# A hybrid decoder layer on one core: the first weight chunk loaded in two parts behind two tiles of x, ScalarE's and VectorE's opening work in another order

## Chip, cores and metric

One NeuronCore of a Trainium2 chip. The metric is the device time of one execution in microseconds; the time before is the median of three runs.

## What is computed

One inference step of a decoder layer, in fp32, for 512 prompt rows and 8 sample rows of width 1024:

```python
xn = rms_norm(x, g_norm_mix)
z = xn @ w_in                      # 1024 x 3072: q 768 | k 768 | v 768 | B 256 | C 256 | u 256
q, k = rope(rms_norm(heads(q), g_q), pos), rope(rms_norm(heads(k), g_k), pos)
# attention over three dilated windows, short convolution of C * u, one output projection
h = x + concat([attn_out, conv_out]) @ w_out
y = h + hier_moe(rms_norm(h, g_norm_ffn))     # top 1 of 4 groups, top 2 of 8 experts, 32 experts
```

The change lies in the first tenth of the time: the norm of x, its transposition, and the first columns of `xn @ w_in`.

## The kernel before

Each engine has its own program, written out by hand; the engines meet at semaphores, and each works strictly in its own order. Names: `pe` is TensorE, `act` ScalarE, `dve` VectorE, `pool` GpSimd, `sp` the queue that issues loads.

**Opening.** x comes as the sample rows (tile NT) and four tiles of 128 rows (0 to 3). For a tile, ScalarE squares and takes the root (`x_square`), VectorE scales (`x_scale`), TensorE transposes eight blocks of 128 x 128 in two halves, VectorE multiplies by the gain out of the bank (`x_whole(g)`). The halves are counted g = 1 to 8, g = 0 being the sample rows: tile t has g = 2t + 1 and 2t + 2. The products are made of two reduced-precision parts: ScalarE copies a part `xT_high` (`x_high(g)`), and the difference `xT_low` is made by VectorE for g = 1 to 4 (`x_low`) and by GpSimd for 5 to 8 (L1811). The difference takes the place of the whole value.

**Projection.** `w_in` is cut into 8 chunks of 384 columns, `wchunk[c]`, loaded in one transfer each. A chunk is split as x is: ScalarE copies `w_high` in four pieces (`high(c, i)`, two of the eight row blocks each), VectorE subtracts to `w_low` (`low(c, i)`), in place over the chunk, so not before `partial_sums(c)` has read it for the sample rows. Per chunk and tile, a unit, TensorE does 16 matmuls with `w_high` (`by_high`, L670 and L671) and 8 with `w_low` (L694). Chunks 0 and 1 are q, 2 and 3 are k. Units of these four go through a norm and rotation: ScalarE squares (L1090), VectorE reduces (L1351), ScalarE roots, VectorE scales and multiplies by the cosine table, GpSimd multiplies by the sine table (L1837) and adds (L1853), TensorE turns the result back (`turn_rot`) three units later. VectorE makes the low pieces of chunk c + 1 between its units of chunk c. The tables `rope_g` hold cosine and sine times the gain, two for q and two for k, and VectorE makes all of them ahead of its first unit (L1337, L1340).

**Sample rows.** `partial_sums(c)` gives sums in four strips that `part_copy` (ScalarE) and `combine` (TensorE) bring together. `turn_state` transposes the convolution's state into bank 4; ScalarE copies it (`cu_s`, L1113) before `combine(0)` writes that bank.

**Loads.** `sp` issues, in this order: sample rows, tile 0, identity, gains, tiles 1 to 3, chunk 0, cosine and sine tables and small constants (`misc_in`), chunks 1 and 2. Later chunks wait for units to be done, and expert weights (L484, L492, L497) for the work that frees their slots.

Of the kernel before, what the change touches and what calls it, by code (L numbers as in the profile page):

```python
# [26 lines left out]
P = 128  # L27
# [10 lines left out]
CW = 384  # L38
# [87 lines left out]
def build(nc, x_prompt, x_sample, cache_k, cache_v, state_conv, g_norm_mix, w_in, g_q, g_k, w_conv, g_attn_out,  # L126
# [3 lines left out]
    with ctx:  # L130
# [119 lines left out]
        def sm(name):  # L250
# [10 lines left out]
        gqk = cut(work, 3200, 2, DH)  # L261
# [42 lines left out]
            y_ready y_out  moved_go dve_link act_link pool_link flag_ready zero_rows gu_front gu_half""".split()  # L304
# [81 lines left out]
        def _(sp):  # L386
# [13 lines left out]
            sp.dma_start(wchunk[0], w_in_v[:, :, 0:CW]).then_inc(w_in_s[0], 16)  # L400
# [134 lines left out]
            half_gates((30, 31), 0, 0, S["gu_front"])  # L535
# [33 lines left out]
        def _(pe):  # L569
# [5 lines left out]
            for g in range(2 * NT + 1):  # L575
                t, half = (g - 1) // 2, (g - 1) % 2
                pe.wait_ge(S["x_scaled"], t + 2)
                if g >= 3:
                    pe.wait_ge(S["x_whole"], g - 2)
                if g == 0:  # L580
                    for k in range(KD):
                        last = pe.transpose(bank[g % 3][:, k * DEC:(k + 1) * DEC], xn[0:DEC, NT, k * P:(k + 1) * P],
                                            ident[0:DEC, 0:DEC])
                else:
                    for k in range(4):
                        o = (4 * half + k) * P
                        last = pe.transpose(bank[g % 3][:, k * P:(k + 1) * P], xn[:, t, o:o + P], ident[:, :])
                last.then_inc(S["x_turned"], 1)
            pe.wait_ge(S["x_whole"], 2 * NT + 1)
# [62 lines left out]
            def partial_sums(c):  # L652

                pe.wait_ge(w_in_s[c % 4], 16 * (c // 4 + 1))
                if c >= 1:
                    pe.wait_ge(S["part_evac"], c)
                for k in range(KD):
# [5 lines left out]
            def by_high(c, t):  # L663
# [3 lines left out]
                if c == 0:  # L667
                    pe.wait_ge(S["x_evac"] if t < 2 else S["x_evac_p"], 2 * (t % 2) + 2)
# [4 lines left out]
            partial_sums(0)  # L673
            pend = []
            for c in range(QKV_CHUNKS):
                pe.wait_ge(S["w_high_done"], 4 * (c + 1))
                if c == 0:
                    by_high(0, 0)
                    by_high(0, 1)
                    turn_state()  # L680
                for t in range(NT):
# [9 lines left out]
                    if t == 0:  # L691
                        pe.wait_ge(S["w_low_done"], 4 * (c + 1))
# [3 lines left out]
                    last.then_inc(S["z_done"], 1)  # L696
                    if t == 0 and c <= 4 or (c, t) == (5, 2):
# [32 lines left out]
            for i in range(6):  # L730
# [11 lines left out]
                if i % 3 == 0:  # L742
                    pe.wait_ge(S["w_low_done"], 4 * (c + 1))
# [141 lines left out]
            def keep_warm(n):  # L885

                for _ in range(n):
                    pe.matmul(bank[2][:, 0:P], ident[:, :], ident[:, :], start=True, stop=True)

# [67 lines left out]
            keep_warm(13)  # L957
            count(2)
            keep_warm(9)
            tabulate(2)  # L960
            keep_warm(16)


            def pair(i, s, turn, first, split=False):
# [6 lines left out]
                pe.wait_ge(*((S["gu_front"], 64) if split else (gu_in[s], loads)))  # L971
# [68 lines left out]
        def _(act):  # L1040
# [16 lines left out]
            def high(c, i):  # L1057

                act.wait_ge(w_in_s[c % 4], 16 * (c // 4 + 1))
# [3 lines left out]
            x_square(NT)  # L1063
            x_square(0)
            x_square(1)
            for t in (2, 3):
                x_high(2 * t - 3)
                x_high(2 * t - 2)
                x_square(t)
            x_high(5)  # L1070
            x_high(6)
            for i in range(4):
                high(0, i)
            x_high(7)
            x_high(8)

            def part_copy(c):
# [3 lines left out]
                act.activation(partial, bank[3][:, 0:CW], ACT.Copy).then_inc(S["part_evac"], 1)  # L1081

# [11 lines left out]
            part_copy(0)  # L1094
            k = 0
            pend = []
            for c in range(QKV_CHUNKS):
                for t in range(NT):
# [11 lines left out]
                    if (c, t) == (0, 0):  # L1110
                        act.wait_ge(S["state_turned"], 1)
                        for h in range(2):
# [845 lines left out]
```

## Time and profile before

| | |
|---|---|
| median of three runs | 631.76 us (626.87 to 632.2) |
| profiled execution | 633.07 us |
| its span | 631.4 us |
| TensorE busy | 87% |
| VectorE, ScalarE, GpSimd busy | 43%, 26%, 18% |
| mean granted clock of TensorE | 0.941 |

A busy share is a mean over the whole span; the opening has other shares than the rest. The span runs from the first to the last instruction, and the execution's own time is somewhat longer.

### The profile page before, as it was taken

What the parts mean: (1) busy time and instruction counts of PE and PEld (TensorE: products, weight loads), DVE (VectorE), ACT (ScalarE), POOL (GpSimd) and SP (SyncE); (2) the same over time, 40 slices, a digit from 0 to 9 for tenths busy, and PEclk for the clock granted to TensorE, in tenths of its full rate; (3) what the DMA queues carried; (4) which work ended last, traced back from release to release, by engine and by line L of the source; (5) the groups of instructions that cost most, each with busy time, mean ns of one, the idle gap of its engine ahead of it and who ended that gap; (6) DMA issues with size and microseconds to landing.
All of it is one profiled execution on the core that took longest, in us unless ns stands there. A gap on an engine that the chain in (4) does not pass through costs nothing.

```text
span 631.4 us, 8032 instructions
## 1 busy us (share of the span) xinstructions
PE 548.1 (87%) x2894; PEld 330.8 (52%) x2894; DVE 271.2 (43%) x628; ACT 161.3 (26%) x357; POOL 113.5 (18%) x126
## 2 busy tenths in 40 slices
PE   3799999998998999899999889999987869787920
PEld 3588899896764887754555743333322323232300
DVE  4876686978313687534266722111210201111117
ACT  5543444423301557520322311010100101000000
POOL 0367788510000000000000131111110111100000
PEclk9699999999999999889999889999997979897985
DMA  7872332589449300049502929999999999999628
GB/s 267 265 195 101 103 137 89 165 244 309 161 125 333 144 1 2 2 195 422 223 33 94 373 70 364 420 418 418 421 421 422 420 419 421 420 422 410 245 75 349
DMA packets 42805, 159.71 MB, mean 253 GB/s; under 512 B 8800, under 2 KB 18080, under 8 KB 30968
## 3 DMA queue, kind: packets, MB, share of 16 engines
q1 hardware_dynamic: 36400, 143.85, 59.9%
q0 software_dynamic: 6368, 15.38, 6.9%
q8 instruction: 21, 0.34, 0.2%
q14 instruction: 16, 0.13, 0.1%
HBM read 151.59 MB, written 16.03 MB: 265 GB/s over the span
## 4 chain that ended last, share of the span: by engine, by line
PE 55%; SPq 17%; DMA 13%; DVE 6%; ACT 3%; issue 2%; POOL 2%; POOLq 0%; DVEq 0%; ACTq 0%
SPq L484 11%; PE bank L976 10%; PE bank L924 9%; SPq L497 5%; DMA ring<-in_w_up_dram 5%; PE bank L1003 4%; PE bank L807 4%; PE bank L694 3%; DMA x<-q_rows 3%; PE bank L670 3%; PE bank L671 3%; PE bank L718 2%; PE bank L792 2%; DMA ring<-results 2%; PE bank L659 2%
## 5 line engine op out<-in xcount | busy, mean ns | idle before, releaser
L976 PE MATMUL bank<-ring,work 128*64 128x512 f32 x512 | 124.3, 642 | 22.7 <-DMA ring<-in_w_up_dram 21.2
L976 PEld LDWEIGHTS bank<-ring,work 128*64 128x64 f32 x512 | 40.0, 148 | 105.1 <-issue 88.0
L1274 DVE TENSOR_TENSOR work<-work,bank 128x256 f32<-128x256 f32 x16 | 6.7, 421 | 140.5 <-ACT work L1243 140.5
L670 PE MATMUL bank<-split 128*128 128x384 f32 x192 | 66.5, 346 | 0.0
L1003 PE MATMUL bank<-ring,work 128*64 128x512 f32 x256 | 58.5, 598 | 7.6 <-ACT work L1247 7.6
L671 PE MATMUL bank<-split 128*128 128x384 f32 x192 | 64.6, 336 | 0.0
L1274 DVE TENSOR_TENSOR split<-ring,split 128x768 fp32r<-128x768 f32 (+1 forms) x36 | 39.6, 1138 | 8.3 <-PE bank L659 8.3
L924 PE MATMUL bank<-ring 128*128 128x512 f32 x96 | 42.6, 594 | 0.0
L1243 ACT ACTIVATE work<-bank 128x256 f32<-128x256 f32 x16 | 6.1, 384 | 140.9 <-PE bank L976 140.9
L1837 POOL TENSOR_TENSOR ring<-ring 128x192 f32<-128x192 f32 (+1 forms) x40 | 37.6, 960 | 17.6 <-DVEq L1362 16.2
L1866 POOL DMA_DIRECT2D hn_rows<-work x5 | 2.7, 543 | 210.6 <-ACT work L1229 210.6
L670 PEld LDWEIGHTS bank<-split 128*128 128x128 f32 x192 | 36.4, 189 | 3.2 <-issue 1.3
L694 PE MATMUL bank<-split 128*128 128x384 f32 x192 | 37.5, 336 | 0.1
L1189 ACT ACTIVATE ring<-ring,st 128x512 f32<-128x512 f32 (+3 forms) x48 | 26.5, 554 | 43.4 <-DVE st L1440 43.4
L1003 PEld LDWEIGHTS bank<-ring,work 128*64 128x64 f32 x256 | 17.0, 136 | 38.8 <-issue 27.4
L671 PEld LDWEIGHTS bank<-split 128*128 128x128 f32 x192 | 36.4, 190 | 0.0
L1888 POOL DMA_INDIRECT results<-work,tbl x16 | 16.1, 1004 | 112.8 <-DVE work L1727 112.8
L1727 DVE COPY work<-bank 128x512 f32<-128x512 f32 x16 | 11.1, 692 | 55.2 <-PE bank L1003 55.2
L694 PEld LDWEIGHTS bank<-split 128*128 128x128 f32 x192 | 33.5, 188 | 1.1 <-issue 0.6
L1880 POOL DMA_INDIRECT work<-hn_rows,tbl x16 | 16.1, 1009 | 98.9 <-PE bank L987 86.8
L1631 DVE SCALAR_TENSOR_TENSOR x<-bank,st,x 128x512 f32<-128x512 f32 (+1 forms) x20 | 15.0, 748 | 37.2 <-PE bank L924 27.6
L807 PE MATMUL bank<-ring 128*128 128x64 f32 x240 | 30.4, 274 | 0.4 <-DVE ring L1274 0.3
(219 smaller groups left out, 808.1 us busy)
## 6 DMA issues: line engine op xcount, KB each, us to landing
ring<-in_w_down_dram SPq DMA_DIRECT2D x32, 1024.0 KB, 24.9
ring<-in_w_gate_dram SPq DMA_DIRECT2D x28, 1024.0 KB, 23.7
ring<-in_w_up_dram SPq DMA_DIRECT2D x28, 1024.0 KB, 25.7
ring<-in_w_in_dram SPq DMA_DIRECT2D x8, 1536.0 KB, 10.4
x<-in_x_prompt_dram SPq DMA_DIRECT2D x8, 512.0 KB, 7.5
ring<-in_w_out_dram SPq DMA_DIRECT2D x1, 4096.0 KB, 12.8
ring<-in_w_gate_dram SPq DMA_DIRECT2D x8, 512.0 KB, 12.1
ring<-in_w_up_dram SPq DMA_DIRECT2D x8, 512.0 KB, 13.7
```

Source lines behind the costliest of these rows:

```text
L484: sp.dma_start(gate_up[s][h][:, o, :, :], w[0, ds(e, 1)].rearrange("e (p k) f -> p (e k) f", p=P)).then_inc(gu_in[s], 16)
L497: sp.dma_start(down[s][h], w_down[0, ds(e, 1)].rearrange("e (p k) n -> p (e k) n", p=P)).then_inc(dn_in[s], 16)
L670: pe.matmul(bank[n % 3][:, 0:CW], xT_high[:, k, cols], w_high[c][:, k, :], start=(k == 0), stop=False)
L671: pe.matmul(bank[n % 3][:, 0:CW], xT_low[:, k, cols], w_high[c][:, k, :], start=False, stop=False)
L694: last = pe.matmul(bank[n % 3][:, 0:CW], xT_high[:, k, cols], w_low[c][:, k, :], start=False, stop=(k == KD - 1))
L807: last = pe.matmul(bank[6 + u % 2][:, h * DH:(h + 1) * DH], probs_t[u % 2][h][:, j * P:(j + 1) * P], v_rows[:, j, (2 * hp + h) * DH:(2 * h ...
L924: last = pe.matmul(bank[g][:, :], src, wout[:, k, cols], start=(k == rng[0]), stop=(k == rng[-1]))
L976: last = pe.matmul(bank[2][64 * h:64 * h + 64, :], xgT[:, k, 64 * h:64 * h + 64], gate_up[s][h][:, :, k, :], start=(k == 0), stop=(k == KD ...
L1003: last = pe.matmul(bank[4 + j][64 * h:64 * h + 64, :], hT[:, c, 64 * h:64 * h + 64], down[s][h][:, c, j * 512:(j + 1) * 512], start=(c == ...
L1189: act.activation(buf, buf, ACT.Exp, bias=nmax[:, u % 4:u % 4 + 1], scale=-1.0, accum_out=den[:, u % 24:u % 24 + 1]).then_inc(S["exp_done"], 1)
L1274: return dve.tensor_tensor(out, a, b, op)
L1837: last = pool.tensor_tensor(sv[:, :, a * half:(a + 1) * half], zv[:, :, b * half:(b + 1) * half], bc(rope_g[2 * (cc // 2) + 1][0:w, t, a * ...
```

## The change

- The first chunk is loaded in two halves of four row blocks each, issued behind tile 1 and ahead of tiles 2 and 3. The first half has the semaphore `front_in`, which later serves in the place of `gu_front`.
- `turn_x` transposes into banks 5 to 7; g = 0 to 4 ahead of the first products, 5 and 6 between the `by_high` of units 0 and 1, 7 behind it, 8 behind the low products of unit 0. Five matmuls (`keep_warm`) stand behind the turn of the gains.
- ScalarE makes the chunk's high pieces between its work on x, and copies the state before it squares unit 0.
- VectorE makes low pieces of chunk 0 between its work on x. The fourth piece is GpSimd's, ahead of its `x_low`; `w_low_done` is then one less everywhere.
- TensorE waits for the high pieces of a chunk one by one.
- The tables for k are made after unit (1, 1) and the sample rows of chunk 1, and `gqk` lies in `rt`, since its old place is written by then.

```diff
-            sp.dma_start(wchunk[0], w_in_v[:, :, 0:CW]).then_inc(w_in_s[0], 16)
+                if t == 1:
+                    for half, loaded in ((0, S["front_in"]), (1, w_in_s[0])):
+                        rows = slice(4 * half, 4 * half + 4)
+                        sp.dma_start(wchunk[0][:, rows, :], w_in_v[:, rows, 0:CW]).then_inc(loaded, 16)
...
+            keep_warm(5, bank[4])
+
+            def turn_x(g):
...
+            for g in range(5):
+                turn_x(g)
             pe.wait_ge(S["pads_zero"], 1)
...
                 for k in range(KD):
+                    if k % 2 == 0 and t == 0:
+                        pe.wait_ge(S["w_high_done"], 4 * c + k // 2 + 1)
...
                 if c == 0:
+                    partial_sums(0)
                     by_high(0, 0)
+                    turn_x(5)
+                    turn_x(6)
                     by_high(0, 1)
+                    turn_x(7)
                     turn_state()
...
                     if t == 0:
-                        pe.wait_ge(S["w_low_done"], 4 * (c + 1))
+                        pe.wait_ge(S["w_low_done"], 4 * (c + 1) - 1)
+                        if c == 0:
+                            pe.wait_ge(S["x_evac_p"], 1)
...
                     last.then_inc(S["z_done"], 1)
+                    if n == 0:
+                        turn_x(8)
...
+            part_copy(0)
+            for g in range(5, 9):
+                x_high(g)
+            act.wait_ge(S["state_turned"], 1)
+            for h in range(2):
+                act.activation(cu_s[:, h, 0:2, :], bank[4][:, h * 16:h * 16 + 16]
+                               .rearrange("p (b j) -> p j b", j=2), ACT.Copy).then_inc(S["cu_ready"], 1)
...
+            rope_tables(0, DH ** -0.5)
+            x_whole(8)
...
+                    if (c, t) == (1, 1):
+                        rope_tables(1, 1.0)
...
+            pool.wait_ge(S["part_done"], 1)
+            pool.wait_ge(S["w_high_done"], 4)
+            pool.tensor_tensor(w_low[0][:, 6:8, :], wchunk[0][:, 6:8, :], w_high[0][:, 6:8, :].bitcast(F32), ALU.subtract)\
+                .then_inc(S["x_evac_p"], 1)
```

ScalarE from the square of tile 1 to the first square of z, before (`ring,st<-x` is `x_square`, `split32768` `xT_high`, `split24576` `w_high`, `work<-bank3` `part_copy`, `ring<-bank4` the copy of the state):

```order
L1046 ACTIVATE ring,st<-x 128x1024 [waits x_in1]
L1047 ACTIVATE st<-st 128x1 [waits act_link]
L1055 ACTIVATE split32768<-ring 128x4x128 [waits x_whole] x2
L1046 ACTIVATE ring,st<-x 128x1024 [waits x_in2]
L1047 ACTIVATE st<-st 128x1 [waits act_link]
L1055 ACTIVATE split32768<-ring 128x4x128 [waits x_whole] x2
L1046 ACTIVATE ring,st<-x 128x1024 [waits x_in3]
L1047 ACTIVATE st<-st 128x1 [waits act_link]
L1055 ACTIVATE split32768<-ring 128x4x128 [waits x_whole] x2
L1060 ACTIVATE split24576<-ring 128x768 [waits w_loaded0] x4
L1055 ACTIVATE split32768<-ring 128x4x128 [waits x_whole] x2
L1081 ACTIVATE work<-bank3 128x384 [waits part_done]
```

The same stretch now, from the first high pieces on:

```order
L1083 ACTIVATE split24576<-ring 128x768 [waits front_in] x2
L1075 ACTIVATE split32768<-ring 128x4x128 [waits x_whole] x2
L1066 ACTIVATE ring,st<-x 128x1024 [waits x_in2]
L1067 ACTIVATE st<-st 128x1 [waits act_link]
L1083 ACTIVATE split24576<-ring 128x768 [waits w_loaded0] x2
L1075 ACTIVATE split32768<-ring 128x4x128 [waits x_whole] x2
L1066 ACTIVATE ring,st<-x 128x1024 [waits x_in3]
L1067 ACTIVATE st<-st 128x1 [waits act_link]
L1090 ACTIVATE work<-bank3 128x384 [waits part_done]
L1075 ACTIVATE split32768<-ring 128x4x128 [waits x_whole] x4
L1110 ACTIVATE ring<-bank4 128x16 [waits state_turned]
L1110 ACTIVATE ring<-bank4 128x16
```

The high pieces moved from behind the square of tile 3 to both sides of the square of tile 2, and the last four `x_high` stand behind the partial sums' copy.

VectorE from the scaling of tile 3 to the first reduce of z, before (`ring<-bank` is `x_whole`, `split28672` `xT_low`, `split0` `w_low`, `SCALAR_TENSOR_TENSOR` the tables):

```order
L1288 TENSOR_SCALAR ring<-x,st 128x1024 [waits dve_link]
L1274 TENSOR_TENSOR ring<-bank2,gains 128x4x128 [waits x_turned]
L1274 TENSOR_TENSOR ring<-bank0,gains 128x4x128 [waits x_turned]
L1274 TENSOR_TENSOR ring<-bank1,gains 128x4x128 [waits x_turned]
L1274 TENSOR_TENSOR ring<-bank2,gains 128x4x128 [waits x_turned]
L1274 TENSOR_TENSOR split28672<-ring,split32768 128x4x128 [waits x_high] x2
L1274 TENSOR_TENSOR split0<-ring,split24576 128x768 [waits w_high_done,part_done] x4
L1337 SCALAR_TENSOR_TENSOR ring<-work 128x320 [waits misc_in]
L1340 SCALAR_TENSOR_TENSOR ring<-work 128x5x32 x2
```

And now:

```order
L1312 TENSOR_SCALAR ring<-x,st 128x1024 [waits dve_link]
L1298 TENSOR_TENSOR split0<-ring,split24576 128x768 [waits w_high_done,part_done] x2
L1298 TENSOR_TENSOR ring<-bank7,gains 128x4x128 [waits x_turned]
L1298 TENSOR_TENSOR ring<-bank5,gains 128x4x128 [waits x_turned]
L1298 TENSOR_TENSOR ring<-bank6,gains 128x4x128 [waits x_turned]
L1364 SCALAR_TENSOR_TENSOR ring<-work,rt 128x320 [waits misc_in]
L1367 SCALAR_TENSOR_TENSOR ring<-work,rt 128x5x32 x2
L1298 TENSOR_TENSOR ring<-bank7,gains 128x4x128 [waits x_turned,rope_ready]
```

Between tile 3 and the first reduce, two low pieces stand where four stood, one pair of tables where two stood, and `x_low` 3 and 4 moved ahead of tile 3's scaling; the last `x_whole` is behind the table.

## Rows read from the trace of the kernel before

**Rows 1.** The DMA view of the moments of issue: KB, us to landing
```profile
x<-in_x_prompt_dram SPq DMA_DIRECT2D x1, 512.0 KB, 3.3
ring<-in_w_in_dram SPq DMA_DIRECT2D x1, 1536.0 KB, 9.7
```
**Rows 2.** Timeline of the SP queue: start us, us, instruction
```profile
3.90 1.30 SPq L393 DMA_DIRECT2D x<-in_x_prompt_dram  x3
5.24 0.43 SPq L400 DMA_DIRECT2D ring<-in_w_in_dram  x1
```
**Rows 3.** Timeline of ScalarE: start us, us, instruction, idle before it
```profile
11.29 0.63 ACT L1055 ACTIVATE split<-ring 128x512 fp32r<-128x512 f32 x1 [1.62 <-DVE ring L1274]
12.62 1.04 ACT L1046 ACTIVATE ring<-x 128x1024 f32<-128x1024 f32 x1
...
22.24 3.03 ACT L1060 ACTIVATE split<-ring 128x768 fp32r<-128x768 f32 x4
...
34.25 0.49 ACT L1090 ACTIVATE ring<-bank 128x384 f32<-128x384 f32 x1 [7.57 <-PE bank L694]
35.66 0.24 ACT L1113 ACTIVATE ring<-bank 128x16 f32<-128x16 f32 x2
```
**Rows 4.** Timeline of VectorE
```profile
14.30 0.75 DVE L1288 TENSOR_SCALAR ring<-x,st 128x1024 f32<-128x1024 f32 x1
14.97 1.28 DVE L1274 TENSOR_TENSOR split<-ring,split 128x512 fp32r<-128x512 f32 x2
...
22.53 0.69 DVE L1274 TENSOR_TENSOR ring<-bank,gains 128x512 f32<-128x512 f32 x1 [0.16 <-PE bank L587]
23.14 2.35 DVE L1274 TENSOR_TENSOR split<-ring,split 128x512 fp32r<-128x512 f32 x2
26.14 5.51 DVE L1274 TENSOR_TENSOR split<-ring,split 128x768 fp32r<-128x768 f32 x4 [0.65 <-PE bank L659]
31.57 0.48 DVE L1337 SCALAR_TENSOR_TENSOR ring<-work 128x320 f32<-128x320 f32 x1
31.97 0.55 DVE L1340 SCALAR_TENSOR_TENSOR ring<-work 128x160 f32<-128x160 f32 x2
...
34.87 0.55 DVE L1351 TENSOR_REDUCE st<-ring 128x6 f32<-128x384 f32 x1 [1.48 <-ACT ring L1090]
...
47.08 2.62 DVE L1274 TENSOR_TENSOR split<-ring,split 128x768 fp32r<-128x768 f32 x2
...
63.82 0.94 DVE L1274 TENSOR_TENSOR split<-ring,split 128x768 fp32r<-128x768 f32 x1
65.02 0.56 DVE L1351 TENSOR_REDUCE st<-ring 128x6 f32<-128x384 f32 x1 [0.27 <-ACT ring L1090]
...
67.36 2.63 DVE L1274 TENSOR_TENSOR split<-ring,split 128x768 fp32r<-128x768 f32 x2
```
**Rows 5.** Timeline of TensorE
```profile
15.11 0.66 PE L587 MATMUL bank<-ident,ring 128*128 128x128 f32 x4 [2.09 <-DVE ring L1288]
...
23.28 2.79 PE L659 MATMUL bank<-ring,work 128*32 128x384 f32 x16 [0.78 <-DVE ring L1274]
...
34.14 1.50 PE L659 MATMUL bank<-ring,work 128*32 128x384 f32 x16
...
49.75 1.66 PE L694 MATMUL bank<-split 128*128 128x384 f32 x8
...
70.36 1.55 PE L694 MATMUL bank<-split 128*128 128x384 f32 x8
```
**Rows 6.** Windows of 2 us: PE, PEld, DVE, ACT, POOL busy, granted clock, DMA
```profile
16.00:18.00 2.00, 1.00 (x4) 0.71 (x4) 1.46 (x3) 1.11 (x2) 0.00 (x0) 0.75 1.01 354
```
**Rows 7.** The chain of waits, in order of time
```profile
27.70 0.18 PE bank L671
```
**Rows 8.** Timeline of GpSimd
```profile
25.86 3.23 POOL L1811 TENSOR_TENSOR split<-ring,split 128x512 fp32r<-128x512 f32 x2 [1.53 <-ACT split L1055]
```
**Rows 9.** Waits of the SP queue: us in total, times, longest
```profile
SPq L484 <- PE bank L924: 61.8, 2, 58.4
```

More of the change, by code:

```diff
@@ L260, in build @@
         gain_in = cut(work, 3072, P)
-        gqk = cut(work, 3200, 2, DH)
+        gqk = cut(rt, 1283, 2, DH)
         state_in = cut(rt, 1026, DC)
@@ L573, in _, with keep_warm @@
             pe.transpose(bank[7][:, 0:30], gain_in[0:30, :], ident[0:30, 0:30]).then_inc(S["gains_turned"], 1)
-            for g in range(2 * NT + 1):
+            def keep_warm(n, where):
+                for _ in range(n):
+                    pe.matmul(where[:, 0:P], ident[:, :], ident[:, :], start=True, stop=True)
+            keep_warm(5, bank[4])
+            def turn_x(g):
                 t, half = (g - 1) // 2, (g - 1) % 2
@@ L586, in _ @@
                         o = (4 * half + k) * P
-                        last = pe.transpose(bank[g % 3][:, k * P:(k + 1) * P], xn[:, t, o:o + P], ident[:, :])
+                        last = pe.transpose(here[:, k * P:(k + 1) * P], xn[:, t, o:o + P], ident[:, :])
                 last.then_inc(S["x_turned"], 1)
-            pe.wait_ge(S["x_whole"], 2 * NT + 1)
+            for g in range(5):
+                turn_x(g)
             pe.wait_ge(S["pads_zero"], 1)
@@ L656, in partial_sums @@
                     pe.wait_ge(S["part_evac"], c)
+                else:
+                    pe.wait_ge(S["front_in"], 16)
+                    pe.wait_ge(S["x_whole"], 1)
                 for k in range(KD):
@@ L970, in pair @@
                 loads = 64 * turn if first or s > 0 else 64 * turn + 64
-                pe.wait_ge(*((S["gu_front"], 64) if split else (gu_in[s], loads)))
+                pe.wait_ge(*((S["front_in"], 80) if split else (gu_in[s], loads)))
                 for k in range(KD):
@@ L1057, in high @@
             def high(c, i):
-                act.wait_ge(w_in_s[c % 4], 16 * (c // 4 + 1))
+                if (c, i) in ((0, 0), (0, 1)):
+                    act.wait_ge(S["front_in"], 16)
+                else:
+                    act.wait_ge(w_in_s[c % 4], 16 * (c // 4 + 1))
                 act.activation(w_high[c][:, 2 * i:2 * i + 2, :], wchunk[c][:, 2 * i:2 * i + 2, :], ACT.Copy)\
                     .then_inc(S["w_high_done"], 1)
[L1063 to L1075, printed above, removed]
             def part_copy(c):
@@ L1081, in part_copy @@
                 act.activation(partial, bank[3][:, 0:CW], ACT.Copy).then_inc(S["part_evac"], 1)
+            x_square(NT)
+            x_square(0)
+            x_square(1)
+            high(0, 0)
+            high(0, 1)
+            x_high(1)
+            x_high(2)
+            x_square(2)
+            high(0, 2)
+            high(0, 3)
+            x_high(3)
+            x_high(4)
+            x_square(3)
+            part_copy(0)
[5 more added lines that the diff above has]
+                               .rearrange("p (b j) -> p j b", j=2), ACT.Copy).then_inc(S["cu_ready"], 1)
             def rot_copy(c, t):
@@ L1316, in _, with rope_tables @@
             x_scale(1)
-            x_whole(1)
-            x_whole(2)
-            for t in (2, 3):
-                x_scale(t)
-                if t == 2:
-                    x_low(1)
-                    x_low(2)
-                x_whole(2 * t - 1)
-                x_whole(2 * t)
-            x_whole(7)
-            x_whole(8)
-            x_low(3)
-            x_low(4)
-            for i in range(4):
-                low(0, i)
+            for g in range(1, 3):
+                x_whole(g)
+            for g in range(1, 3):
+                x_low(g)
+            for g in range(3, 5):
+                x_whole(g)
+            x_scale(2)
+            low(0, 0)
+            for g in range(3, 5):
+                x_low(g)
+            x_scale(3)
+            low(0, 1)
+            low(0, 2)
+            x_whole(5)
+            x_whole(6)
+            x_whole(7)
             dve.wait_ge(S["misc_in"], 128)
             half = DH // 2
-            for i, scale in ((0, DH ** -0.5), (1, 1.0)):
+            def rope_tables(i, scale):
                 g = gqk[:, i, :]
@@ L1748, in _ @@
                 link = S["rope_ready"]
-                at = [1]
+                at = [2]
                 def lstep(ins):
```

38 lines of the change are left out of this document (14 added, 24 removed).

## The prediction

> **What bounds the kernel now.** I read the chain of waits first, then the timelines of the engines over its first 50 us, then the same engines one chunk later, then what the DMA queue waits for. The execution has a span of 631.4 us and took 633.07 us; 1.7 us lie around the span, and the median of the three timed runs, 631.76 us, is 1.3 us lower. The reader is to see three things.
>
> First, TensorE does no matrix work of the projection until 26.0 us. It transposes x in short bursts and waits in between for tiles that go ScalarE (square, root), VectorE (scale), TensorE (turn), VectorE (`x_whole`), ScalarE (`x_high`), VectorE or GpSimd (`x_low`). Tile 2 is squared at 12.62, two `x_high` follow, and the first weight pieces (`high`, four in 3.03 us) start only at 22.24 [rows 3], though the first chunk landed at 5.24 + 9.7 = 14.9 us [rows 1, 2]. The matmuls of `partial_sums(0)` start at 23.28 and take 2.79 us, against 1.50 us for the same work at 34.14 [rows 5]: the granted clock fell from 2.4 to 1.2 GHz in the window from 16 to 18 us, where it is 0.75 on average [rows 6], and nearly the double time says that it was still down at 23. A matmul of `by_high` takes 0.18 us at 27.70 [rows 7].
>
> Second, after 26 us TensorE is the bound: its first low products of chunk 1 start at 49.75 and those of chunk 2 at 70.36 [rows 5], one chunk in 20.6 us. VectorE is close behind. The reduce that opens its z work starts at 34.87, and the last two low pieces of chunk 1 end at 47.08 + 2.62 = 49.70, the moment at which TensorE goes on; for chunk 2 they end at 67.36 + 2.63 = 69.99 [rows 4], 0.37 us ahead of it. So 14.8 us pass on VectorE from its first reduce to the release of chunk 1, whatever TensorE could do.
>
> Third, later loads are issued relative to TensorE's progress: the queue waited 61.8 us for L924 before expert weights [rows 9]. A stage that starts earlier moves everything behind it; I found no wait on something that comes at a fixed time.
>
> **Loads.** From x tile 1, which lands at 3.90 + 3.3 = 7.2, to the chunk at 14.9, tiles 2 and 3 and the chunk arrive, 2.62 MB in 7.7 us, so 340 GB/s [rows 1, 2]. With the order changed the first half lands at about 9.5, the second at 11.8, tile 2 at 13.4, tile 3 at 14.9. One more issue costs SP 0.43 us [rows 2], hidden since the queue is behind anyway. The small tables come at most that much later than now and are first wanted after 22 us.
>
> **ScalarE.** `high(0, 0)` and `(0, 1)` fit in the idle 1.62 us ahead of the first `x_high` [rows 3]: two by 0.76 = 1.5 us from 9.7, free. `x_high` 1 and 2 end at 12.7, as now. Square 2 must wait for its tile: 13.4 in place of 12.62, a loss of 0.8. From a square's start to the end of the scaling it allows is 14.30 + 0.75 - 12.62 = 2.43 us [rows 3, 4], of which ScalarE has less than 14.30 - 12.62 = 1.7; I take 1.5. So ScalarE: 14.9; two `high`, 16.4; two `x_high` of 0.63 each, 17.7; square 3 starts at 17.7 and tile 3 is scaled at 20.1. That is about where it is now, since square 3 is behind the weights. The profit is that the weights' high parts are done at 16.4 and not at 25.3.
>
> **TensorE.** The turns of tiles 0 and 1 end at 13.0 as now. `partial_sums(0)` 1.5, to 14.5. `by_high(0, 0)` waits for `high` piece by piece, ends at about 17.2. Turns 5 and 6, 0.66 each [rows 5], 18.5. `by_high(0, 1)` needs `x_low(4)`, which VectorE gives 1.2 us behind `x_high(4)`, at 18.9; 16 by 0.175 [rows 7] = 2.8, to 21.7. Turn 7 and the state, 22.7. `w_low` of chunk 0: VectorE makes pieces 1 and 2 after scaling tile 3, 2 by 0.95 to 22.0 (alone; 1.38 each in the row beside GpSimd [rows 4]), and GpSimd's piece is 768 wide where its row has 512 in 3.23 / 2 = 1.6 us [rows 8]: 2.4 us from 16.4, long done. Low products of unit 0, 1.66 [rows 5], end at 24.3, turn 8 at 25.0. What follows is the same stream as now from 34.14 to 49.75, 15.6 us [rows 5]: TensorE could begin the low products of chunk 1 at 40.6, 9.1 us earlier than now.
>
> **VectorE, which decides.** After `low(0, 2)` at 22.0: `x_whole` 5, 6, 7 at 0.69 [rows 4], 24.1; the tables for q, three instructions, 31.97 + 0.55 - 31.57 = 0.95 [rows 4], 25.0; `x_whole(8)`, 25.7. ScalarE: `x_high(8)`, 0.6; the state's copies, 0.24; then the first square of z, 0.49 [rows 3]: 27.0. GpSimd makes its four `x_low` from 23.4 to 29.8 in this time. Rows bound what this costs VectorE: an `x_low` pair took 1.28 us alone and 2.35 us beside GpSimd, while an `x_whole`, which reads a bank, took 0.69 beside it as well [rows 4, 8]. Only the table has two such inputs, so 0 to 0.8; I take 0.4, nearest to a single pair's loss per instruction. First reduce at 27.5 in place of 34.87: **7.4 us earlier**. Adding the unchanged 14.8 gives 42.3 for the release of chunk 1. TensorE, ready at 40.6, waits 1.7 us there. This is the new wait, and 7.4 us is what the first stage gives, not 9.1.
>
> The Trainium skill, "SBUF — State Buffer", section "Who interferes with whom", says that a VectorE instruction with two SBUF inputs and a GpSimd instruction that reads SBUF exclude each other: whichever comes second waits for the whole of the other. By that, each of the table's three instructions could wait for an `x_low` of GpSimd, not only share with it; the sum would be about 2 us smaller. The pairs above (1.28 against 2.35) agree that there is a loss, and cannot tell how it adds up over three short instructions.
>
> **The keys' table, moved.** Its 0.95 us leave the path ahead of the first reduce (counted above) and come back behind unit (1, 1). Queued behind it are unit (1, 2) and the last low pieces of chunk 2, for which TensorE has 0.37 us to spare [rows 4, 5]; the idle 0.27 us ahead of the reduce at 65.02 [rows 4] is all else. 0.95 - 0.64 = 0.3 lost, 0.7 if GpSimd is beside it. GpSimd wants it only at chunk 2.
>
> **State copies** move ahead of the first square, 0.24, counted. Five warm-up matmuls lie in the wait between the gains and x, 1.25 us at most where 2 us are free: nothing. The finer `w_high_done` waits, other banks and the place of `gqk` cost nothing that rows show.
>
> **Sum.** 7.4 - 0.3 = 7.1, less 0.1 for waits added in TensorE's stream: 7.0 us. Against the profiled execution 633.07 - 7.0 = 626.1; against the median 631.76 - 7.0 = **624.8 us**. Bounds of the unknowns: landing of tile 2 0.5 either way, the table 0 to 0.8, keys' table 0 to 0.7: 5.5 to 8.5 us, so 623.3 to 626.3.
>
> **Rivals.** *The shared reads cost more* (0.10). VectorE is behind GpSimd not only in the table but in `low(0, 0)` and `x_low` 3 and 4, and the whole chain slips 3 us: for it, 5.51 us for four low pieces that alone take 0.95; against it, GpSimd's first piece runs while VectorE waits for square 3. 628 us.
>
> *The clock stays low for a while* (0.07). The last three turns now stand behind matmuls, so VectorE's `x_whole(8)` hangs on TensorE's pace. If the clock falls at 17 us as now, 24 matmuls and three turns before turn 8 cost double, 5 to 6 us more: 630 us. For it: the granted clock did fall there [rows 6]. Against it: it fell when TensorE had done only one burst of 0.66 us between 13 and 17 us [rows 5], where it now has `partial_sums` and `by_high`. The skill, "TensorE: Matmul & The Clock Gate", "What's actually happening", has the slow level as the default that activity releases; by that the denser start keeps 2.4 GHz, and the trace agrees in that the clock came back after matmuls had run from 23.28 on.
>
> *Nothing arrives at the end* (0.06): 631.8 us. A later stage might have held the time anyway, the expert loads above all. Against it [rows 9]: those loads wait for TensorE.
>
> *Slower* (0.04). The same low clock, but lasting: from the first partial sums to the release of chunk 1 TensorE has 25 us of work at full rate and reached 49.75 in 36.7 us before. With about 2 us of waits it loses when more than some 20 us run at half clock, from 17 to 37. The low stretch was 10 us before. If it lasts to 45 us, 13 us are added to 27 and the time is about 635 us.
>
> *More than foreseen* (0.03): tile 2 lands with the halves and TensorE has no wait: 621.
>
> **Numbers.** The forecast has 0.70. A change of this kernel under 1% (6.3 us, below 625.4 is faster by more) can't be told from none. Of the 0.70 I put 0.52 below that, since 7.0 is near it; with the last case 0.55 faster. Same: 0.18, the lock, the clock's milder case and no gain, 0.41. Slower 0.04. The range for 8 in 10 reaches from 620.5 to 630.5: it leaves out the slower case, no gain, and half of the best.
>
> **What would show it.** `partial_sums(0)` at about 13; granted clock 1.00 from 12 to 30; first z reduce at 27 to 28; low products of chunk 1 at 42 to 43 after a wait for VectorE's low pieces; those of chunk 2 about 21 us later; the span shorter by as much. The prediction is wrong if tile 2 lands after 15 us, if the clock drops in the first `by_high`, or if a wait behind 50 us grows.

## The result, and the profile after

Fifteen executions each of the kernel before and the changed one, beside each other, gave medians of 632.12 and 627.80 us. The ratio is 0.9944, with a 95% interval of 0.9921 to 0.9968: the changed kernel is faster by 0.56%, 3.5 us (2.0 to 5.0). Another set of executions, told as the ninth experiment, gave 0.9949. The forecast was 7.0 us. The ratio is worked out over the fast executions (one of the changed kernel, at 666.91 us, was in the slow state) and not from the two medians, which are 4.3 us apart. The profiled execution took 631.91 us with a span of 630.2 us and a mean granted clock of 0.942, only 1.2 us under the one before; the last part of the experiments says what is particular to this one execution.

The loads, as issued from 0 to 20 us (KB, median us to landing); the two halves of the weights are the group of two:

```profile
x<-in_x_prompt_dram SPq DMA_DIRECT2D x4, 512.0 KB, 5.7
ring<-in_w_in_dram SPq DMA_DIRECT2D x2, 768.0 KB, 6.5
```

ScalarE (start, duration, what, idle before it and its releaser), which answers to [rows 3]:

```profile
10.04 1.58 ACT L1083 ACTIVATE split<-ring 128x768 fp32r<-128x768 f32 x2 [0.38 <-DMA ring<-in_w_in_dram]
...
13.43 1.06 ACT L1066 ACTIVATE ring<-x 128x1024 f32<-128x1024 f32 x1 [0.73 <-DMA x<-in_x_prompt_dram]
...
14.81 1.57 ACT L1083 ACTIVATE split<-ring 128x768 fp32r<-128x768 f32 x2
...
17.32 1.04 ACT L1066 ACTIVATE ring<-x 128x1024 f32<-128x1024 f32 x1
```

All four high pieces are done at 16.38 us, where the old kernel ended them at 25.27 [rows 3]. Tile 2 is squared at 13.43 and tile 3 at 17.32. The copies of the state stand behind the last `x_high`, and `combine(0)` waits for them. TensorE, which answers to [rows 5]:

```profile
12.95 2.23 PE L676 MATMUL bank<-ring,work 128*32 128x384 f32 x16
...
23.33 1.66 PE L717 MATMUL bank<-split 128*128 128x384 f32 x8
24.83 0.60 PE L599 MATMUL bank<-ident,ring 128*128 128x128 f32 x4
...
29.51 0.81 PE L624 MATMUL bank<-work,small 128*8 128x384 f32 x2 [1.04 <-ACT ring L1110]
...
44.55 2.40 PE L717 MATMUL bank<-split 128*128 128x384 f32 x8 [2.60 <-DVE split L1298]
46.88 2.33 PE L676 MATMUL bank<-ring,work 128*32 128x384 f32 x16
...
67.28 1.67 PE L717 MATMUL bank<-split 128*128 128x384 f32 x8 [0.39 <-DVE split L1298]
68.88 1.50 PE L676 MATMUL bank<-ring,work 128*32 128x384 f32 x16
```

The last turn of x is at 24.83 us. The low products of chunk 1 start at 44.55 instead of 49.75, 5.2 us ahead; those of chunk 2 at 67.28 instead of 70.36, only 3.1 us ahead. So 2.1 us are given back between the two chunks. There the same work takes longer: eight low products 2.40 us against 1.67 at 67.28, sixteen partial sums 2.33 against 1.50. Windows of that stretch (length, busy us of PE, PEld, DVE, ACT and POOL, granted clock, DMA share, GB/s) show why:

```profile
44.00:45.00 1.00, 0.45 (x2) 0.45 (x3) 0.96 (x2) 0.01 (x1) 1.00 (x1) 1.00 1.06 373
45.00:46.00 1.00, 1.00 (x5) 1.00 (x5) 0.64 (x2) 0.67 (x2) 0.36 (x1) 0.60 1.05 369
46.00:47.00 1.00, 1.00 (x7) 0.56 (x10) 0.67 (x2) 0.01 (x1) 0.76 (x1) 0.50 0.57 193
47.00:48.00 1.00, 1.00 (x8) 0.28 (x12) 0.42 (x1) 0.48 (x1) 0.87 (x3) 0.50 0.03 12
48.00:49.00 1.00, 1.00 (x12) 0.19 (x4) 0.60 (x3) 0.30 (x1) 0.84 (x1) 0.69 0.00 0
49.00:50.00 1.00, 1.00 (x10) 0.86 (x7) 0.84 (x2) 0.27 (x1) 0.57 (x1) 1.00 0.00 0
```

TensorE waited 2.60 us for VectorE's low pieces, began again at 44.55, and from about 45.2 to 48.6 us its clock was granted at 1.2 GHz (the means of 0.60 and 0.69 are windows with the change in them). VectorE, which answers to [rows 4]:

```profile
20.39 1.82 DVE L1298 TENSOR_TENSOR split<-ring,split 128x768 fp32r<-128x768 f32 x2
22.13 1.88 DVE L1298 TENSOR_TENSOR ring<-bank,gains 128x512 f32<-128x512 f32 x3
23.92 1.27 DVE L1364 SCALAR_TENSOR_TENSOR ring<-work,rt 128x320 f32<-128x320 f32 x1
25.11 2.71 DVE L1367 SCALAR_TENSOR_TENSOR ring<-work,rt 128x160 f32<-128x160 f32 x2
27.86 0.69 DVE L1298 TENSOR_TENSOR ring<-bank,gains 128x512 f32<-128x512 f32 x1
29.84 0.55 DVE L1381 TENSOR_REDUCE st<-ring 128x6 f32<-128x384 f32 x1 [1.29 <-ACT ring L1120]
...
41.89 2.60 DVE L1298 TENSOR_TENSOR split<-ring,split 128x768 fp32r<-128x768 f32 x2
...
60.19 0.94 DVE L1298 TENSOR_TENSOR split<-ring,split 128x768 fp32r<-128x768 f32 x1
61.05 0.47 DVE L1364 SCALAR_TENSOR_TENSOR ring<-work,rt 128x320 f32<-128x320 f32 x1
61.46 0.54 DVE L1367 SCALAR_TENSOR_TENSOR ring<-work,rt 128x160 f32<-128x160 f32 x2
```

And GpSimd, which answers to [rows 8], in the same stretch and at the table for k (one instruction alone):

```profile
23.55 4.09 POOL L1847 TENSOR_TENSOR split<-ring,split 128x512 fp32r<-128x512 f32 x3 [5.09 <-ACT split L1075]
...
59.84 2.61 POOL L1873 TENSOR_TENSOR ring<-ring 8x192 f32<-8x192 f32 x1 [0.17 <-DVEq L1392]
```

The table for q takes from 23.92 to 27.82 us, 3.9 us for three instructions that took 0.95 in the old kernel [rows 4] and take 0.95 for k at 61.05. GpSimd's three `x_low`, 1.36 us each on the mean, 23.55 to 27.64, lie on exactly this stretch. Taken one by one, they end at 24.84, 26.32 and 27.64, and the three instructions of the table at 25.19, 26.51 and 27.83: each of them ends 0.2 to 0.35 us behind an `x_low`. At 61.05 GpSimd isn't idle either. There it stands in a multiplication by the sine table from 59.84 to 62.45, VectorE works without a gap from 59.71 to 62.00, and GpSimd is the one that waits: the same instruction takes 1.74 us in the second and the fifth experiment, where no table stands beside it. So which of the two waits isn't a matter of the instruction alone. The three `x_whole` just ahead, each of which reads a bank, take 1.88 us together, 0.63 each, though GpSimd already works under the third.

**Two causes can be read here**: a table that is slowed by GpSimd and holds up everything on VectorE behind it, and a clock that falls behind TensorE's wait. The experiments separate them.

### The profile page after: what moved, and what is told of

It reads as the page before. It is cut to its first block, busy times and chain, and to the rows that moved or that the text cites. A ratio compares the mean times of both kernels' runs of the same rounds, so it can differ in the third digit from the quotient of the medians.

```text
span 630.2 us, 8056 instructions
## 1 busy us (share of the span) xinstructions
PE 551.4 (88%) x2904; PEld 335.2 (53%) x2904; DVE 271.8 (43%) x627; ACT 161.1 (26%) x357; POOL 116.0 (18%) x127
## 4 chain that ended last, share of the span: by engine, by line
PE 60%; DMA 14%; SPq 12%; DVE 7%; ACT 3%; issue 3%; POOL 0%; POOLq 0%; DVEq 0%; ACTq 0%
PE bank L996 11%; PE bank L944 9%; DMA ring<-in_w_up_dram 9%; SPq L487 8%; PE bank L717 4%; PE bank L1023 4%; PE bank L689 4%; PE bank L690 4%; PE bank L832 3%; PE bank L743 2%; PE bank L817 2%; SPq L500 2%; DVE split L1298 2%; DMA ring<-results 2%; DMA x<-in_cache_v_dram 2%
## 5 line engine op out<-in xcount | busy, mean ns | idle before, releaser
L996 PE MATMUL bank<-ring,work 128*64 128x512 f32 x512 | 121.6, 630 | 22.3 <-DMA ring<-in_w_up_dram 20.8
L1023 PE MATMUL bank<-ring,work 128*64 128x512 f32 x256 | 58.5, 598 | 7.6 <-ACT work L1271 7.6
L1298 DVE TENSOR_TENSOR split<-ring,split 128x768 fp32r<-128x768 f32 (+1 forms) x35 | 37.2, 1097 | 8.4 <-PE bank L676 8.1
```

What stands on the lines that cost most here:

```text
L996: last = pe.matmul(bank[2][64 * h:64 * h + 64, :], xgT[:, k, 64 * h:64 * h + 64], gate_up[s][h][:, :, k, :], start=(k == 0), stop=(k == KD ...
L1023: last = pe.matmul(bank[4 + j][64 * h:64 * h + 64, :], hT[:, c, 64 * h:64 * h + 64], down[s][h][:, c, j * 512:(j + 1) * 512], start=(c == ...
L1298: return dve.tensor_tensor(out, a, b, op)
```

## The experiments

In the table stand, for each kernel, the start of the first z reduce on VectorE, the start of the low products of chunk 1 with TensorE's wait ahead of them in brackets, the same of chunk 2, and the ratio to the kernel before with its 95% interval. All starts are of the profiled execution, in us.

| kernel | first reduce | chunk 1 (wait) | chunk 2 | ratio |
|---|---|---|---|---|
| before | 34.87 | 49.75 | 70.36 | |
| changed | 29.84 | 44.55 (2.60) | 67.28 | 0.9944 [0.9921, 0.9968] |
| 1, table early | 27.21 | 42.03 (1.42) | 63.21 | 0.9877 [0.9837, 0.9916] |
| 2, both tables early | 27.54 | 42.94 (2.29) | 65.09 | 0.9895 [0.9859, 0.9931] |
| 3, fillers in the wait | 29.50 | 44.22 (0.38) | 65.39 | 0.9885 [0.9845, 0.9924] |
| 4, GpSimd later | 27.41 | 42.56 (1.81) | 65.25 | one execution, 631.52 us |
| 5, early, k's in a gap | 27.09 | 41.93 (1.43) | 62.56 | 0.9885 [0.9827, 0.9942] |
| 6, the same with fillers | 27.05 | 41.89 (0.33) | 62.49 | 0.9848 [0.9794, 0.9902] |
| 7, weights last | 31.72 | 46.43 (2.60) | 69.12 | one execution, 635.39 us |
| 8, no warm-ups | 29.46 | 44.17 (2.60) | 66.94 | one execution, 631.40 us |
| 9, changed, again | 29.47 | 44.19 (2.60) | 66.89 | 0.9949 [0.9916, 0.9982] |
| 10, as 3, again | 29.49 | 44.21 (0.38) | 65.39 | 0.9900 [0.9867, 0.9933] |
| 11, as 1, again | 27.11 | 41.93 (1.42) | 63.10 | 0.9888 [0.9842, 0.9934] |

**1. The table for q ahead of GpSimd's work.** It moves to a place at which GpSimd has no `x_low` to make yet.

```diff
             low(0, 2)
+            rope_tables(0, DH ** -0.5)
             x_whole(5)
             x_whole(6)
             x_whole(7)
-            rope_tables(0, DH ** -0.5)
             x_whole(8)
```

> The kernel after, with the q tables made right after low(0, 2), while GpSimd has nothing to do, and x_whole 5 to 8 behind them. Theory (the tables were slow, 3.94 us, because they stood beside GpSimd's x_low): the three instructions take 0.95 us as in the kernel before, the first reduce of z starts at 27.5 to 27.9 in place of 29.84, the low products of chunk 1 at 42.2 to 42.8 in place of 44.55, the wait ahead of them falls from 2.6 to under 1 us, and the clock stays at 2.4 GHz there. The span up to chunk 2 is 3.5 to 4.5 us shorter than after. Rival (the tables are slow by themselves in this kernel, for instance since the gains now lie in rt): they take 3.9 us here too, and nothing before 44 us moves forward. Against the kernel before 7 us faster by the theory, 3 to 4 by the rival.

VectorE in the first experiment:

```profile
21.88 0.49 DVE L1360 SCALAR_TENSOR_TENSOR ring<-work,rt 128x320 f32<-128x320 f32 x1
22.29 0.56 DVE L1363 SCALAR_TENSOR_TENSOR ring<-work,rt 128x160 f32<-128x160 f32 x2
22.88 1.89 DVE L1298 TENSOR_TENSOR ring<-bank,gains 128x512 f32<-128x512 f32 x3
```

The same three instructions take 0.97 us, and the first reduce comes 2.6 us earlier, 0.3 us ahead of what was expected. TensorE is ready at 42.03 - 1.42 = 40.6 us, waits 1.42 us (expected: under 1), and goes on at its full clock: chunk 2 is 21.2 us behind chunk 1, against 22.7 in the changed kernel. That is 7.15 us ahead of the kernel before, and the median of 622.22 us against 630.25 is 8.0 us ahead. At chunk 2 three instructions moved ahead of three others are worth another 4.1 us, more than the 3.1 of the whole change.

**4. The same test from the other side.** Order on VectorE stays, and GpSimd holds its `x_low` back until the table is made.

```diff
+            pool.wait_ge(S["rope_ready"], 1)
             for g in range(5, 9):
```

> The kernel after, with one wait more on GpSimd: its four x_low start only when the q tables are made; the tables stay where they are. Theory (shared reads): the tables take 0.95 us from 23.9, x_whole(8) ends at 26.1 or when turn 8 lets it, the first reduce starts at 27.5 to 28, though GpSimd's x_low end later, at 30 to 31. Rival (tables slow by themselves): 3.9 us as after.

VectorE in the fourth experiment:

```profile
23.84 0.48 DVE L1364 SCALAR_TENSOR_TENSOR ring<-work,rt 128x320 f32<-128x320 f32 x1
24.24 0.55 DVE L1367 SCALAR_TENSOR_TENSOR ring<-work,rt 128x160 f32<-128x160 f32 x2
```

Here the table stands where it stands in the changed kernel and takes 0.95 us. So it is GpSimd's `x_low` beside it that makes it 3.9 us, and nothing in its place or its inputs. The first reduce is at 27.41, as the forecast had it, but the clock still falls:

```profile
42.56 2.83 PE L717 MATMUL bank<-split 128*128 128x384 f32 x8 [1.81 <-DVE split L1298]
45.32 1.86 PE L676 MATMUL bank<-ring,work 128*32 128x384 f32 x16
```

Chunk 2 is 22.7 us behind chunk 1, as in the changed kernel. The single execution took 631.52 us and decides nothing on the whole time.

**2. Both tables early.** The tables for k leave the stretch behind unit (1, 1) as well.

```diff
             low(0, 2)
+            rope_tables(0, DH ** -0.5)
+            rope_tables(1, 1.0)
             x_whole(5)
...
-                    if (c, t) == (1, 1):
-                        rope_tables(1, 1.0)
```

> As e1, with the k tables made in the same place too, as before the change. Theory: both take 1.9 us; the first reduce is 0.95 later than in e1 and the release of chunk 1 with it; in return the wait of 0.39 us ahead of the low products of chunk 2 is gone. Level with e1 within 1 us at the end. Rival (making the k tables later is where the gain comes from): 2 us or more slower than e1 from chunk 2 on.

The first reduce is 0.33 us later than in the first experiment, the release of chunk 1 at 42.94 is 0.9 us later, and TensorE's wait is 2.29 us with the clock down behind it. At chunk 2 TensorE no longer waits. The 0.40 us that the tables for k cost at chunk 2 are bought with 0.9 us at chunk 1 and a clock fall. Chunk 2 starts 1.9 us later than in the first experiment and the median, 624.16 us, is 1.9 us higher: more than the 1 us of the theory, which had no fall in it, and just under the 2 us of its rival.

**3. Fillers in TensorE's wait.** Ten matmuls on the identity, into a bank that the next turn overwrites, stand in the wait. The work of every engine is otherwise that of the changed kernel.

```diff
                     if t == 0:
+                        if c == 1:
+                            keep_warm(10, bank[6])
                         pe.wait_ge(S["w_low_done"], 4 * (c + 1) - 1)
```

> The kernel after, with ten idle matmuls of the identity (into bank 6, read by nobody) in TensorE's wait for the low pieces of chunk 1. Theory (the wait of 2.6 us let the clock fall, and this cost another 1.6 us): the low products still start at 44.5 to 44.8, but take 1.66 us and the partial sums behind them 1.5, and unit (1, 2) ends 1.5 us earlier than after. Rival (the slow matmuls there have another cause, contention with the loads): they stay at 2.40 and 2.33 us.

TensorE in the third experiment (each filler has two rows):

```profile
41.45 2.39 PE L581 MATMUL bank<-ident 128*128 128x128 f32 x20
44.22 1.67 PE L719 MATMUL bank<-split 128*128 128x384 f32 x8 [0.38 <-DVE split L1300]
45.81 1.50 PE L676 MATMUL bank<-ring,work 128*32 128x384 f32 x16
```

And its windows:

```profile
46.00:47.00 1.00, 1.00 (x16) 0.26 (x8) 0.86 (x2) 0.41 (x1) 1.00 (x2) 1.00 1.02 363
47.00:48.00 1.00, 1.00 (x10) 0.76 (x7) 0.60 (x3) 0.47 (x2) 0.87 (x2) 1.00 0.48 174
```

The low pieces still end at 44.2, but everything behind runs at full clock: from the start of the first low products of chunk 1 to that of its last, at 60.33, are 16.11 us, against 44.55 to 62.23, 17.68 us, in the changed kernel. The loads are as dense here (a DMA share of 1.02 in the first window, at a granted clock of 1.00), so they aren't what made those matmuls slow. The fall costs 1.57 us, and the table's delay stays.

**5 and 6. What is left to gain.** The fifth has the table for q early and those for k one unit earlier, behind unit (1, 0). The sixth adds five fillers ahead of the low products of chunk 1 and seven in a wait of 1.84 us at about 147 us, ahead of `turn_scores`.

```diff
-                    if (c, t) == (1, 1):
+                    if (c, t) == (1, 0):
                         rope_tables(1, 1.0)
...
+                        if c == 1:
+                            keep_warm(5, bank[6])
...
                     combine(6)
+                    keep_warm(7, bank[6])
                     turn_scores()
```

> e1 with the k tables made one unit earlier, behind unit (1, 0), where VectorE idled for 3.5 us in the kernel before. Theory (the 0.40 us wait ahead of the low products of chunk 2 is the k tables' time on a full VectorE): that wait goes, those products start 20.8 us behind those of chunk 1 and not 21.2, and everything behind is 0.4 us earlier than in e1. Rival (the 0.40 us has another cause): it stays.

> e5 with idle matmuls of the identity in two waits of TensorE: five ahead of the low pieces of chunk 1 (a wait of 1.4 us), seven ahead of turn_scores (a wait of 1.84 us, the same in all kernels so far). Theory (short waits in TensorE let the clock fall in some executions, 1.6 us each time): the wait ahead of turn_scores is never followed by slow matmuls, its next low products start 4.0 us behind it and not 5.6, the mean time is up to 1 us below e5 and the scatter smaller. Rival (it makes no difference, since e1 and e3 had no slow matmuls there without it): level with e5.

In both there is no wait at chunk 2, 20.6 us behind chunk 1, and 7.8 to 7.9 us are gained by then. At the end the fifth, 0.9885, isn't ahead of the first, 0.9877. The sixth has the best ratio of the study, 0.9848, with a median of 623.79 us against 625.16 of the fifth. In its profile the clock doesn't fall behind the filled wait, as it does in the fifth; but in the profiles of the first and the third it doesn't fall there without fillers either. Its interval overlaps those of the first and the fifth, so that it is the best of the three isn't shown. It is faster than the changed kernel, whose intervals, 0.9921 to 0.9968 and 0.9916 to 0.9982, lie above 0.9902.

**7 and 8. The order of loads, and the warm-ups.** The seventh issues both halves of the weights behind x (`t == NT - 1`), so behind tiles 2 and 3 as in the kernel before, and keeps everything else of the change; the eighth leaves out the five matmuls behind the gains.

```diff
-                if t == 1:
+                if t == NT - 1:
                     for half, loaded in ((0, S["front_in"]), (1, w_in_s[0])):
```

```diff
-            keep_warm(5, bank[4])
```

> The kernel after with the load order of before: both halves of the chunk behind tiles 2 and 3. Tells what the order of the loads is worth, all else as after. Theory (ScalarE's opening order needs the early halves): the first half lands at 12.5 to 13, ScalarE stands there with x_high 1 and 2 behind it, so square 2 starts at 15.7 and not 13.4, and the first reduce is 2.3 to 3.5 us later than after, at 32 to 33; the time is back within 1 us of the kernel before. Rival (the first stage is bound by the tables, the order of loads is hidden): first reduce within 1 us of 29.84.

> The kernel after without the five warm-up matmuls behind the turn of the gains. Theory (they do nothing, the turns behind them ran at the same 3.68 us for 16 as before the change): partial_sums starts at 12.95 and takes 2.2 us, by_high follows at full rate. Rival (they bring the clock up earlier): partial_sums takes 2.8 us and the first by_high matmuls 0.32 us each, which costs 1 to 2 us at unit 0.

ScalarE in the seventh stands in line for the weights:

```profile
12.30 1.58 ACT L1083 ACTIVATE split<-ring 128x768 fp32r<-128x768 f32 x2 [2.57 <-DMA ring<-in_w_in_dram]
```

Its first reduce is 1.88 us later than that of the changed kernel and chunk 2 starts 1.84 us later (2.25 and 2.23 against the ninth, which is the changed kernel once more). So the order of the loads is worth about 2 us, somewhat less than expected: the second square starts at 14.82 and not at 15.7, and the first reduce, at 31.72, is just under the range. With the old order of loads the first reduce is still 3.15 us ahead of the kernel before, and this comes from the rest of the change, above all the order of work on the engines. In the eighth all is as in the changed kernel; 0.3 us are no more than executions differ here (the ninth is at 66.89). The warm-ups are worth nothing in the profile and cost nothing. Both are single executions and say nothing on the whole time.

**9, 10 and 11. The three that matter, on one chip.** The profiles could have shown falls of the clock that most executions don't have. So the changed kernel, the third and the first experiment ran again, beside twenty executions of the kernel before.

> The changed kernel as it is, beside the two that follow on the same chip, so that what the traces show can be compared with timed executions. Both theories expect the low products of chunk 1 at 44.5 behind a wait of 2.6 us, and a time 3 to 4 us under the kernel before (ratio 0.994).

> The changed kernel with ten filler matmuls in TensorE's wait ahead of the low products of chunk 1, once more, on the same chip as the changed kernel. If the clock falls behind that wait in most executions, the timed median is 1.5 us or more under that of the changed kernel (ratio to the kernel before about 0.991 or less). If the fall in the profiled execution was a chance of that execution, the two medians agree within 0.5 us.

> The changed kernel with the queries' table made ahead of x_whole 5 to 7, on the same chip. If the table beside GpSimd and the longer wait that it causes are the whole of what the forecast missed, the timed median is about 4 us under that of the changed kernel and 7 to 8 us under the kernel before (ratio 0.988). If the rest lies in the later part of the kernel, it gains no more than the 2.5 us of the chunk's release.

Medians of 628.91, 626.06 and 623.94 us, against 631.75: gains of 2.8, 5.7 and 7.8 us. The fillers are worth 2.9 us of timed executions and the early table 5.0. Drawing anew from the listed executions leaves 0.2 to 5.7 us for the fillers and 1.6 to 7.8 for the table: both are clear of zero, and their sizes are loose. Ahead at chunk 2, in the profiles, are 3.5, 5.0 and 7.3 us: within that scatter, what is won by 70 us comes out at the end, about one to one.

**What the clock does elsewhere** explains why single profiles differ by more. In the third and the tenth, one kernel, TensorE waits 1.84 us ahead of the same instruction. Their windows from 152 to 156 us, first the third:

```profile
152.00:154.00 2.00, 2.00 (x10) 1.66 (x10) 1.09 (x5) 0.62 (x3) 0.00 (x0) 1.00 1.00 287
154.00:156.00 2.00, 2.00 (x11) 1.65 (x10) 0.74 (x3) 1.45 (x2) 0.00 (x0) 1.00 1.01 336
```

and the tenth:

```profile
152.00:154.00 2.00, 2.00 (x7) 1.61 (x7) 1.09 (x5) 0.63 (x3) 0.00 (x0) 0.66 1.04 309
154.00:156.00 2.00, 2.00 (x6) 1.51 (x6) 0.74 (x3) 1.44 (x2) 0.00 (x0) 0.50 1.02 345
```

The low products behind start at 155.74 in the one and at 157.34 in the other: 1.6 us by chance of the execution. In all, the clock fell behind this wait (1.84 us in most, 2.87 at the longest) in ten of the twelve profiles in which it isn't filled.

A second such place is a wait for the cached values of attention at about 190 us. Its length goes with the landing of a load. In the changed kernel's first profile it was 3.64 us and the clock fell behind it; in the ninth, the same kernel, it was 1.47 us, and in the kernel before 2.63, both without a fall. Here, too, the fourth and the seventh (3.64 and 3.53 us) have the fall, and the fifth and the tenth (2.65 and 2.54 us) have not. The first profile of the changed kernel was 2.96 us ahead of the kernel before at the wait of 1.84 us (153.23 against 156.19), 1.9 us ahead behind the wait for the values (194.29 against 196.19), and 0.35 us ahead 4 us later (198.55 against 198.90). Further falls differ between the two executions too: it was 3.0 us behind at 369 us and 1.0 ahead at 583, and ended 1.2 us ahead. So a single profile says little of the end.

At chunk 1, on the other hand, profile and kernel agree in every case: behind waits of 2.60 (four times), 2.29 and 1.81 us the clock fell, behind 1.42 and 1.43 (three times) and the filled ones (three times) it didn't.

## Why the prediction was wrong

**The table beside GpSimd is the step that failed.** "Only the table has two such inputs, so 0 to 0.8; I take 0.4, nearest to a single pair's loss per instruction." It lost 3.9 - 0.95 = 3.0 us, far over the upper end. The error is in the form of the bound. I took the loss of a pair of `x_low`, 1.07 us, as spread over its two instructions, and so as something that goes with VectorE's own work. Singly, in the trace of the kernel before, with GpSimd's pair beside them:

```profile
21.82 2.51 POOL L1811 TENSOR_TENSOR split<-ring,split 128x512 fp32r<-128x512 f32 x2 [21.21 <-ACT split L1055]
23.14 1.74 DVE L1274 TENSOR_TENSOR split<-ring,split 128x512 fp32r<-128x512 f32 x1
24.80 0.68 DVE L1274 TENSOR_TENSOR split<-ring,split 128x512 fp32r<-128x512 f32 x1
```

The first took 1.74 us and the second 0.68. The whole loss lies in the first, which ended at 24.88, 0.55 us behind the end of GpSimd's second at 24.33; the second had no GpSimd beside it and lost nothing. It is a wait for the rest of GpSimd's instruction, once for each VectorE instruction that meets one. A row of the same view, read one instruction at a time, had it before the change. The table met three, and each of its instructions waited, however short it is. The rule that the prediction set beside it, from the Trainium skill, "SBUF — State Buffer", section "Who interferes with whom", says that the second of the two waits for the whole of the first. The trace agrees: 3.90 us beside three `x_low` of GpSimd, 0.97 and 0.95 us without them, in either way of parting them. The prediction's sum by that rule, about 5.0 us, would have been nearer than 7.0. The first reduce came at 29.84 and not at 27.5, and since 14.7 us still pass to the release of chunk 1 (forecast 14.8), that came at 44.55 and not 42.3. This is 2.2 us of the 4.0 that are missing at chunk 2 (a start at 67.28, where the forecast has 63.3). In the first experiment, where the table costs what it cost before, the reduce is at 27.21, TensorE is ready at 40.6 to the tenth as forecast, and the gain is 7.15 us at chunk 2.

**"TensorE, ready at 40.6, waits 1.7 us there. This is the new wait"** had the wait, and counted it at its own length. It was 2.60 us, and a fall of the clock came with it, 1.57 us more. The wait was longer than forecast although TensorE itself was late, ready at 44.55 - 2.60 = 41.95: `combine(0)` had stood 1.04 us for the state's copies, which come behind `x_high(8)` and so behind the table. I had weighed the clock for the stretch from 17 us, where it never fell (1.00 in every window from 16 to 40 us), and not for the wait that I had myself forecast. This was not among the rivals. The fourth experiment, with a wait of 1.81 us, has the fall too; the first, with 1.42, has not. The forecast wait of 1.7 lies between, and I can't say what it would have done.

**The rival of the shared reads** had the right mechanism in the wrong place, and its time of 628 us by chance, since 1.6 us of what is missing is the clock's. Beyond the table it named `low(0, 0)` and `x_low` 3 and 4. The first took 0.95 us, undisturbed; the pair did lose, 2.68 us from 16.93 on beside GpSimd's `w_low`, against 1.28 alone (again the first alone, 2.08 us, which ended 0.55 us behind GpSimd's 18.46), but tile 3 was still scaled at 20.47, 0.4 us behind the forecast. **The rival of the low clock** was wrong in its stretch. **That nothing arrives at the end** fell: by the tenth and eleventh the later stages pass it on.

**What held.** The loads: tile 2 squared at 13.43 (forecast 13.4), high pieces done at 16.38 (16.4), tile 3 scaled at 20.47 (20.1), low pieces at 22.2 (22.0). TensorE: turn 8 at 24.83 to 25.4 (25.0). The tables for k: a wait of 0.39 us at chunk 2 (0.3), which vanishes in the fifth; with GpSimd beside it, for which the forecast had 0.7, it lost nothing, since there GpSimd waited. The warm-ups: at nothing, rightly, though they take 2.5 us and not "1.25 us at most"; the eighth shows that they are covered. The partial sums were late by half (2.23 us against "1.5", behind a turn at 0.23 us a matmul, where the later ones have 0.13, so at the lower clock, though the clock column has 1.00 there) and without effect, since the second pair of high pieces was made only at 14.81 to 16.38.

The two missed terms and 0.1 for the tables of k make 3.9 of the 4.0 us. That the end then lacks 3.5 us of the forecast, by the timed executions, fits this within their interval.

## What to carry to other kernels

When an instruction is moved, look at what the other engines do at its new place. Short VectorE instructions that read two inputs from SBUF, set beside a row of GpSimd's that do so too, are to be priced at one GpSimd instruction each, not at a share of their own length; where VectorE is the one that works without a gap, GpSimd may pay instead. Before pricing from a row that groups two instructions, look at them singly: a mean of two hid here that one had lost everything. A wait that a change opens on TensorE may cost more than its length, for the clock can fall behind it; fillers in the wait, or a shorter wait, gave that back here. And where one profile ends 2 us from what its own stages say, compare single stages and repeat the timing before looking for a cause.

## What the runs showed of the hardware that was not expected

- Three VectorE instructions of 0.48, 0.31 and 0.31 us on SBUF took 3.90 us beside GpSimd's 128x512 subtractions, and 0.95 to 0.97 without; each ended 0.2 to 0.35 us behind one of GpSimd's. Three `x_whole`, of which one input is a bank, took 1.88 us, with GpSimd working under the third.
- It goes the other way too. Where VectorE had the low piece and the three of the table in a row, a GpSimd multiplication of 8x192 took 2.61 us, and 1.74 where the three of the table weren't among them; VectorE's kept their length.
- After waits of 1.81 to 2.60 us at chunk 1, with TensorE busy before and after, the clock went to 1.2 GHz only after work had begun again (in the changed kernel work began at 44.55, and the clock was down from about 45.2 to 48.6). It isn't the length alone: behind a wait of 1.84 us at one place of one kernel it fell in one execution and not in another (the third and the tenth), and at about 190 us it fell behind 3.53 and 3.64 us, but not behind waits up to 2.65. The Trainium skill, "TensorE: Matmul & The Clock Gate", "What's actually happening", says that the point at which the level changes varies between runs of one kernel. The traces agree and show more: between executions of one kernel the fall can come or stay away, low products behind it starting at 157.34 or 155.74 us.
- The last load of the cached values landed between 7.2 and 10.2 us after its issue, by execution, and two profiles of the changed kernel waited for it 3.64 and 1.47 us.
